# Second mixer: the logarithm of the keys is added to the sums of log gates, so that one exponential gives the decayed keys, and GpSimd has no work there

## The reference, cut to what matters

```python
fq, f_fwd, f_bwd, fi, fog = _split(h @ w_in, ODD_SIZES)
q = _heads(jax.nn.silu(fq), HGRN_HEADS)
for d, f in enumerate((f_fwd, f_bwd)):
    log_f = jnp.logaddexp(jnp.log(lb[d]), jnp.log1p(-lb[d]) + jax.nn.log_sigmoid(_heads(f, HGRN_HEADS)))
    k = -jnp.expm1(log_f)
    dirs.append(_directional_scan(q, k, i, log_f, n_ctx, reverse=(d == 1)))
...
G = jnp.cumsum(gc, axis=2)                     # in _chunk_gla, gc = log_f
decay = jnp.exp(jnp.where(tri, G[:, :, :, None, :] - G[:, :, None, :, :], -jnp.inf))
scores = jnp.einsum('bhik,bhjk,bhijk->bhij', qc, kc, decay)
```

## Time and profile before

| | |
|---|---|
| median of 3 runs | 2525.53 us (2525.48 to 2527.56) |
| span of the profiled execution, first to last instruction | 2523.3 us |
| the difference, what lies around the span | 2.2 us, taken against the median, since the profiled execution has no other time of its own |
| PE, DVE, ACT, POOL busy over the span | 92%, 60%, 42%, 9% |
| the eight heads of the changed stage | 885 to 1175 us of the span |
| mean granted TensorE clock | 0.970 of 2.4 GHz |

### The profile page before, as it was taken

The page is one execution under the profiler, slowest core; times in us unless marked ns, Lnnn a source line. Parts: engine busy times, 40 slices in busy tenths (PEclk is TensorE's granted clock), DMA queues, the critical chain, the costliest instruction groups (busy, mean ns, idle before and its releaser), DMA issues.

```text
span 2523.3 us, 35620 instructions
## 1 busy us (share of the span) xinstructions
PE 2326.2 (92%) x14882; PEld 1850.7 (73%) x14882; DVE 1510.6 (60%) x2358; ACT 1068.3 (42%) x1808; POOL 224.7 (9%) x302
## 2 busy tenths in 40 slices
PE   6987788999998988887999997988999999998999
PEld 3854456888885867766999782336888888878999
DVE  6337655656565487777555515554666565995554
ACT  4244444322234445554445525544332333444543
POOL 0001200000000033322000002110110200000110
PEclk9988988999999999998999999999999999999999
DMA  7154542444432454433554223342444434434453
GB/s 276 68 210 167 213 187 86 142 142 157 159 117 84 134 167 159 142 134 105 187 181 168 77 88 134 134 167 86 142 142 156 145 123 184 177 131 156 168 200 118
DMA packets 175280, 372.80 MB, mean 148 GB/s; under 512 B 8432, under 2 KB 101872, under 8 KB 160784
## 3 DMA queue, kind: packets, MB, share of 16 engines
q1 hardware_dynamic: 175120, 370.53, 42.2%
HBM read 340.07 MB, written 30.44 MB: 147 GB/s over the span
## 4 chain that ended last, share of the span: by engine, by line
PE 75%; DVE 11%; ACT 7%; issue 3%; DMA 2%; POOL 1%; SPq 0%; DVEq 0%; ACTq 0%; POOLq 0%
PE ps L169 74%; DVE sb_R L200 3%; ACT sb_R L252 2%; DVE sb_WP L200 1%; PE ps L179 1%; DVE sb_cst L214 1%; ACT sb_R L258 1%; DVE sb_H L200 1%; DVE sb_cst L200 1%; ACT L245 1%; DMA sb_slot<-mod_w 1%; DVE sb_R L229 1%; DMA sb_slot<-even_w_in 1%; DVE sb_X L217 1%; DVE sb_R L217 1%
## 5 line engine op out<-in xcount | busy, mean ns | idle before, releaser
L169 PE MATMUL ps<-sb_HP,sb_WP 128*128 128x512 f32 (+1 forms) x5736 | 1084.6, 350 | 32.7 <-DVE sb_HP L200 27.6
L169 PEld LDWEIGHTS ps<-sb_HP,sb_WP 128*128 128x128 f32 x5736 | 920.7, 192 | 180.4 <-DVE sb_HP L200 24.6
L200 DVE TENSOR_TENSOR sb_WP<-sb_slot,sb_WP 128x1024 fp32r<-128x1024 f32 x380 | 471.5, 1245 | 593.6 <-ACT sb_WP L258 593.3
L258 ACT ACTIVATE sb_WP<-sb_slot 128x1024 fp32r<-128x1024 f32 x380 | 399.8, 1058 | 724.4 <-PE ps L169 709.3
L169 PE MATMUL ps<-sb_XP,sb_WP 128*128 128x256 f32 (+1 forms) x2976 | 498.2, 330 | 0.3 <-DVE sb_XP L200 0.3
L169 PEld LDWEIGHTS ps<-sb_XP,sb_WP 128*128 128x128 f32 x2976 | 446.0, 191 | 51.8 <-DVE sb_XP L200 0.7
L200 POOL TENSOR_TENSOR sb_R<-sb_R 128x128 f32<-128x128 f32 (+2 forms) x194 | 159.8, 847 | 1546.3 <-ACT sb_R L252 1267.1
L200 DVE TENSOR_TENSOR sb_R<-sb_R 128x256 f32<-128x256 f32 (+3 forms) x398 | 201.2, 540 | 34.1 <-ACT sb_R L252 31.1
L169 PE MATMUL ps<-sb_R 128*32 128x64 f32 (+7 forms) x1768 | 161.4, 288 | 53.8 <-DVE sb_R L200 26.0
L169 PEld LDWEIGHTS ps<-sb_R 128*32 128x32 f32 (+4 forms) x1768 | 113.2, 154 | 110.4 <-issue 68.9
L252 ACT ACTIVATE sb_R<-ps 128x512 f32<-128x512 f32 (+1 forms) x208 | 99.6, 513 | 88.1 <-PE ps L169 83.8
(11 more groups left out here) (149 smaller groups left out, 1863.5 us busy)
## 6 DMA issues: line engine op xcount, KB each, us to landing
sb_slot<-mlp_w SPq DMA_DIRECT2D x32, 2048.0 KB, 8.8
sb_slot<-mod_w SPq DMA_DIRECT2D x22, 2048.0 KB, 8.9
sb_R<-ada_w SPq DMA_DIRECT2D x12, 2048.0 KB, 7.6
sb_slot<-ada_w SPq DMA_DIRECT2D x24, 1024.0 KB, 4.9
sb_slot<-ffn_w_gate SPq DMA_DIRECT2D x22, 1024.0 KB, 5.5
sb_slot<-ffn_w_up SPq DMA_DIRECT2D x22, 1024.0 KB, 8.0
sb_slot<-ffn_w_down SPq DMA_DIRECT2D x10, 2048.0 KB, 7.9
sb_slot<-odd_w_in SPq DMA_DIRECT2D x32, 512.0 KB, 7.3
```

What stands on the lines that cost most here:

```text
L169: return self.e.matmul(out, w, x, start=start, stop=stop, skip_group_check=True)
L200: return BLANK if self.e is None else self.e.tensor_tensor(out, a, b, op)
L258: return self.e.activation(out, a, ACT.Copy) if scale is None else self.e.activation(out, a, ACT.Copy, scale=scale)
```

## The change

The keys of a head are no longer multiplied by an exponential. Since k exp(x) = exp(ln k + x), the logarithm of the keys is made once a head and folded into the sum: K = F - ln k forwards, K = F + ln k backwards. `split_dve` and `keys_dve` subtract K where they subtracted F for the keys, and Exp gives the decayed key itself. In parts:

1. POOL: `keys_pool` of `Levels` (14 multiplications of 128x128 a head) and of `Across` (2 of 128x512 a head) are gone; POOL has no instruction in the stage.
2. ACT: two more activations of 128x512 a head, Ln of the keys with p0 as scale and 2^-60 as bias, behind Ln of the gates.
3. DVE: two more 128x512 subtractions or additions a head (K), behind the two scans and ahead of level 0. The two `tensor_scalar` that make k run over 256 tokens in place of 512, and stand one step earlier, beside the gates. V is written into E's second half.
4. Waits: PE's diagonal blocks wait for k and q, no more for the scans. PE's products wait for E and V in place of U and V; the X multiplications wait for ACT's exponential in place of POOL's product. E has three buffers in turn, freed by the products of three levels before.
5. Small tables (`ex`, `pr`, `mx`) move to another place in memory; a constant is added.

```diff
-            self.levels.append(Levels(p, h, b1, S["q"], ks, S["F"], 2, 2, 1.0, heads, bufs, 3, 5, ready))
-            self.across.append(Across(p, h, b2, S["q"], ks, S["F"], 2, 2, 1.0, WW, QQ, heads, (2, 3), 3, 5))
+            self.levels.append(Folded(p, h, b1, S["q"], ks, S["F"], S["K"], 2, 2, heads, bufs, 3, 5, ready))
+            self.across.append(AcrossFolded(p, h, b2, S["q"], S["F"], S["K"], 2, 2, WW, QQ, heads, (2, 3), 3, 5))
...
+    def diagonal_pe(self, pe):          # Folded
+        nc, tag = self.nc, self.tag
+        pe.wait_ge("k", tag, 1, of="odd.proj")
+        pe.wait_ge("q", tag, of="odd.proj")
...
+    def products_pe(self, pe, m):
+        tag, E = self.tag, self.buf(m)
+        pe.wait_ge("E", tag, m)
+        pe.wait_ge("V", tag, m)
...
+    def split_dve(self, dve, n):
...
+        if n >= 3:
+            self.used(dve, n - 3)
...
+        far = K[:, 0, 0:1, 0:1].offset - F[:, 0, 0:1, 0:1].offset
+        mid = both(F[:, 0, c0, L - 1:L], Fd + 1, [0, L])
+        dve.sub(both(E[:, 0, 0:1], Ez, [1, L]), mid, both(K[:, 0, c0, 0:1], Fd - far, [1, L]))
+        i = dve.sub(both(E[:, 1, L:L + 1], -Ez, [1, L]), both(F[:, 0, c0, L:L + 1], Fd + far, [1, L]), mid)
...
+    def queries_dve(self, dve, m):
+        E = self.buf(m)
+        dve.wait_ge("E", self.tag, m)
+        dve.mul(E[:, 1, :], self.q, E[:, 1, :]).then_inc(*dve.sig("V", self.tag, m))
...
+            act.wait_ge("togo", self.tag, s)          # AcrossFolded.keys_act
+            act.act(w, w, ACT.Exp).then_inc(*act.sig("W", self.tag, s))
...
         e.act(self.g, self.g, ACT.Ln).then_inc(*e.sig("ln", h))
+        for d in range(2):
+            K = S["K"][:, d]
+            e.wait_ge("k", h, d)
+            e.act(K, K, ACT.Ln, scale=self.pr[:, 2 * d, h:h + 1], bias=self.p.v("tiny")).then_inc(*e.sig("lnk", h, d))
...
+        for d in range(2):
+            F, K = S["F"][:, d], S["K"][:, d]
+            e.wait_ge("lnk", h, d)
+            e.wait_ge("F", h, d)
+            (e.sub if d == 0 else e.add)(K, F, K).then_inc(*e.sig("K", h, d))
...
-        pool.on("odd.in").fence(*self.before)
-        for h in range(8):
-            together(self.levels[h].pool(pool.on("odd.mix")), self.cross_pool(pool, h))
+        pass
```

More of the change, by code:

```diff
@@ L1674, in crossed, with __init__, buf, decay_act @@
         e.wait_ge("crossed", self.tag, h, len(self.groups(h)) - 1)
+class Folded(Levels):
+    def __init__(self, p, tag, before, q, ks, F, K, c0, nc, heads, bufs, lo, hi, ready):
+        super().__init__(p, tag, before, q, ks, F, c0, nc, 1.0, heads, bufs, lo, hi, ready)
+        self.K, self.off = K, 0 if before is None else before.off + self.N
+    def buf(self, m):
+        return self.bufs[(self.off + m) % 3]
+    def diagonal_pe(self, pe):
+        nc, tag = self.nc, self.tag
+        pe.wait_ge("k", tag, 1, of="odd.proj")
+        pe.wait_ge("q", tag, of="odd.proj")
+        (pb, sz, P, dg), = self.heads
+        b, ps = pe.take(self.lo, self.hi)
+        for c in range(nc):
+            cs = slice(128 * c, 128 * c + 128)
+            for d, kk in enumerate(dg):
+                i = pe.mm(ps[:, cs], kk[:, cs], self.q[:, cs], d == 0, d == len(dg) - 1)
+        i.then_inc(*pe.sig("diag", tag, 0, bank=b))
+        pe.until(b, "P", tag, -1, 0)
+    def products_pe(self, pe, m):
+        tag, E = self.tag, self.buf(m)
+        pe.wait_ge("E", tag, m)
+        pe.wait_ge("V", tag, m)
+        b, ps = pe.take(self.lo, self.hi)
+        for c in range(self.nc):
+            cs = slice(128 * c, 128 * c + 128)
+            i = pe.mm(ps[:, cs], E[:, 0, cs], E[:, 1, cs], True, True)
+        i.then_inc(*pe.sig("prod", tag, m, 0, bank=b))
+        pe.until(b, "P", tag, m, 0)
+    def decay_act(self, act, n):
+        E = self.buf(n)
+        act.wait_ge("split", self.tag, n)
+        act.act(E, E, ACT.Exp).then_inc(*act.sig("E", self.tag, n))
+    def split_dve(self, dve, n):
+        tag, nc, c0 = self.tag, self.nc, self.c0
+        L, E, F, K = LEVELS[n], self.buf(n), self.F, self.K
+        if n >= 3:
+            self.used(dve, n - 3)
+        elif self.before is not None:
+            self.before.used(dve, self.N - 3 + n)
+        both = lambda x, step, w: bass.AP(x.tensor, x.offset, [list(x.ap[0]), [step, 2], [2 * L, 64 * nc // L], w])
+        Fd, Ez = F.ap[1][0], E.ap[1][0]
+        far = K[:, 0, 0:1, 0:1].offset - F[:, 0, 0:1, 0:1].offset
+        mid = both(F[:, 0, c0, L - 1:L], Fd + 1, [0, L])
+        dve.sub(both(E[:, 0, 0:1], Ez, [1, L]), mid, both(K[:, 0, c0, 0:1], Fd - far, [1, L]))
+        i = dve.sub(both(E[:, 1, L:L + 1], -Ez, [1, L]), both(F[:, 0, c0, L:L + 1], Fd + far, [1, L]), mid)
+        i.then_inc(*dve.sig("split", tag, n))
+    def queries_dve(self, dve, m):
+        E = self.buf(m)
+        dve.wait_ge("E", self.tag, m)
+        dve.mul(E[:, 1, :], self.q, E[:, 1, :]).then_inc(*dve.sig("V", self.tag, m))
@@ new lines, with __init__, keys_dve, keys_act @@
+class AcrossFolded(Across):
+    def __init__(self, p, tag, before, q, F, K, q0, nq, W, Q, heads, chunks, lo, hi):
+        super().__init__(p, tag, before, q, None, F, q0, nq, 1.0, W, Q, heads, chunks, lo, hi)
+        self.K = K
+    def keys_dve(self, dve):
+        self.free(dve)
+        for s in range(2):
+            F, K, w = self.F[:, s], self.K[:, s], self.W[s]
+            w3, end = w.rearrange("p (c x) -> p c x", c=4), (F[:, :, 127:128] if s == 0 else F[:, :, 0:1]).broadcast_to([w.shape[0], 4, 128])
+            (dve.sub(w3, end, K) if s == 0 else dve.sub(w3, K, end)).then_inc(*dve.sig("togo", self.tag, s))
+        for s in range(2):
+            w, x, e = self.W[s], self.W[2 + s], self.W[4 + s]
+            K = lambda c: w[:, 128 * c:128 * c + 128]
+            if s == 0:
+                seq = ((0, K(0), 1), (1, K(1), 2), (2, x[:, 0, :], 2))
+            else:
+                seq = ((0, K(1), 0), (1, K(0), 3), (2, x[:, 0, :], 3))
+            yield
+            dve.wait_ge("W", self.tag, s)
+            dve.wait_ge("whole", self.tag, s)
+            for j, a, b in seq:
+                if j == 2:
+                    dve.wait_ge("X", self.tag, s, 0)
+                dve.ts(x[:, j, :], a, e[:, b:b + 1], ALU.mult).then_inc(*dve.sig("X", self.tag, s, j))
+    def keys_act(self, act):
+        self.free(act)
+        for s in range(2):
+            F, w, e = self.F[:, s], self.W[s], self.W[4 + s]
+            act.wait_ge("togo", self.tag, s)
+            act.act(w, w, ACT.Exp).then_inc(*act.sig("W", self.tag, s))
+            act.act(e, F[:, :, 127 if s == 0 else 0], ACT.Exp, scale=1.0 if s == 0 else -1.0).then_inc(*act.sig("whole", self.tag, s))
@@ L2259, in __init__ @@
         place = Place(p.room, 8192, p.NW - 4096)
-        self.ex, self.pr, self.mx = place(4, 8), place(4, 8), place(2, 8)
-        self.sets = [dict(q=place(TC), og=place(TC), k=place(2, T), F=place(2, 4, 128)) for _ in range(2)]
+        late = Place(lambda at, *shape: shaped(p.cst, at, NCST, shape), NCST - 80)
+        self.ex, self.pr, self.mx = late(4, 8), late(4, 8), late(2, 8)
+        self.sets = [dict(q=place(TC), og=place(TC), k=place(2, TC), F=place(2, 4, 128), K=place(2, 4, 128)) for _ in range(2)]
         self.sg, self.g = place(T), place(2, T)
-        bufs = [(place(2, TC), place(TC), place(TC)) for _ in range(2)]
+        bufs = [place(2, TC) for _ in range(3)]
         PB = place(4 * TC)
```

18 lines of the change are left out of this document (6 added, 12 removed).

## The result

| | before | changed | ratio, 95% interval |
|---|---|---|---|
| first comparison, median of 4 and 4 runs | 2526.55 us (2525.48 to 2528.09) | 2491.86 us (2489.76 to 2501.28) | 0.9895 [0.9873, 0.9918] |
| the same two programs again, 11 and 6 runs | 2517.6 us (2514.51 to 2525.65) | 2500.0 us (2493.19 to 2501.72) | 0.9916 [0.9899, 0.9933] |
| profiled execution, span | 2523.3 us | 2488.0 us, and 2496.9 again | |

The account below looks back on a forecast made before the run. PE and DVE were taken to bound the kernel by waiting for each other in turn. Savings of 6 x 2.4 + 2.0 + 1.65 = 18.05 us took the median from 2525.53 to 2507.5 us, 8-in-10 range 2500 to 2517.

Parts of the forecast that it names:

- S: End of a head's scans on DVE, the zero point for its times; 994.20 us in head 3 before the change.
- p0: PE's products of level 0; forecast at S+4.5 without a stall, or in some heads after a 0.9 us wait.
- p5: PE's products of level 5; forecast 2.5 us earlier, taken as 2.4 a head, with the stretch to the next S unchanged.
- Its central trust: On DVE, the X multiplications are slow because POOL works beside them; the forecast hangs on this.
- lone product: Level 0's query product on DVE, 0.62 us for 0.4; said not to fit the rule of shared ports.
- by rule or by row: Whether the port-blocking rule or the trace's undisturbed durations are used, the forecast sum was claimed to be the same.
- the 1.11: Time in us of the second three X multiplications on DVE, taken as undisturbed; the first three were to fall to it from 2.15.
- Levels 3 to 5: DVE's later levels: 3 and 4 keep their pace and move by 2.0 us; level 5's three products take 1.08 for 1.74.
- p2: PE's products of level 2, set by DVE; forecast to come 1.85 us earlier.
- Another cause for DVE's slowness: Rival, chance 0.08: DVE is not slowed by POOL, K costs 1.3 us and nothing is won; 2525 us.
- the split's subtractions cost more: Rival, chance 0.08: DVE's twelve subtractions reading K and F by a far step each cost 0.26 us more; 2531 us.
- ACT late with the logarithms: Rival, chance 0.05: Ln of the keys ends late, K waits 1 us a head, 8 us are lost; 2515 us.

Follow-up runs that it names:

- the idle POOL work: Changed kernel plus POOL multiplications of constants, in the old ones' places, that nobody reads or waits for; 2522.56 us, ratio to before 1.0012.

## Why the prediction was right, and where it was short

**Direction and mechanism: right.** POOL has no instruction in the stage. The K pair takes 1.27 us (forecast 1.3). The two logarithms of the keys took 1.51 us, more than 2 x 0.63, but ended at 973.08, ahead of S at 974.04. The wait ahead of X is one on ACT, 0.69 (forecast about 0.5). In head 3 p0 comes without a wait, at S + 4.26 (S + 4.5); in head 4, where the matrix-times-vector work stands behind it, p0 comes at S + 3.46 (S + 3.5) behind a wait of 1.07 (0.9). The diagonals do not wait for the scans. From p5 to the next S there are 12.75 us (unchanged, 12.81). In head 7, the wait for the zeros grew from 1.63 to 2.69 in one profile and to 3.69 in the other.

**Its central trust: right, and more so than it says.** "The X multiplications being slow because of POOL" is shown by the idle POOL work, which brings the slowness back without any wait. The Trainium skill, page "SBUF — State Buffer", section "Who interferes with whom", says that the ports shared by VectorE and GpSimd are an exclusive lock. The trace of the kernel before agrees, once the groups of a timeline are taken apart into single instructions. First an X multiplication, then level 0's query product, then a weight remainder and two of level 5's three instructions of 128x256, each beside POOL's instruction:

```profile
1003.70 1.30 POOL L200 TENSOR_TENSOR sb_cst<-sb_cst,sb_R 128x512 f32<-128x512 f32 x1
1003.75 1.34 DVE L214 TENSOR_SCALAR sb_cst<-sb_cst 128x128 f32<-128x128 f32 x1
...
995.80 0.47 POOL L200 TENSOR_TENSOR sb_R<-sb_R 128x128 f32<-128x128 f32 x1 [12.34 <-ACT sb_R L252]
995.92 0.62 DVE L200 TENSOR_TENSOR sb_R<-sb_R 128x256 f32<-128x256 f32 x1
...
1013.45 1.22 DVE L200 TENSOR_TENSOR sb_WP<-sb_slot,sb_WP 128x1024 fp32r<-128x1024 f32 x1
1013.61 1.44 POOL L200 TENSOR_TENSOR sb_R<-sb_R 128x128 f32<-128x128 f32 x1 [2.55 <-ACT sb_R L252]
1014.59 0.74 DVE L200 TENSOR_TENSOR sb_R<-sb_R 128x256 f32<-128x256 f32 x1
1015.01 0.70 POOL L200 TENSOR_TENSOR sb_R<-sb_R 128x128 f32<-128x128 f32 x1
1015.25 0.74 DVE L200 TENSOR_TENSOR sb_R<-sb_R 128x256 f32<-128x256 f32 x1
```

The X multiplication ends 0.08 us behind POOL's instruction, and takes 1.34 where it takes 0.28 alone. Of the 48 in the eight heads 40 began while POOL was at work, and every one ended 0.08 to 0.09 us behind the POOL instruction that was running; the other 8 took 0.27 to 0.28. The query product (0.41 alone) ends 0.28 behind POOL's, and so do both of level 5's. It goes the other way as well: POOL's instruction at 1013.61 ends 0.38 behind the weight remainder that had begun before it, and the one at 1015.01 as much behind the DVE instruction at 1014.59. So the prediction read its lone product wrongly. It said that the rule does not fit, "since POOL was busy much longer than the 0.2 lost"; but the product was held by one POOL instruction, up to 996.26, and not by the pair. It also says that by rule or by row the sum is the same. Laid on every row of POOL, the rule would have marked the 1.11 as disturbed.

**The step that was mis-sized:** "It then takes 1.11 in place of 2.15" and "Levels 3 to 5. Nothing is added; levels 3 and 4 keep their pace." Both took rows of before as undisturbed which POOL disturbed as well; of the 1.11 the prediction says outright "with POOL idle". It was at work at just these places, as its timeline in the kernel before shows:

```profile
1006.50 0.88 POOL L200 TENSOR_TENSOR sb_R<-sb_R 128x128 f32<-128x128 f32 x2 [1.49 <-ACT sb_R L252]
1010.00 1.06 POOL L200 TENSOR_TENSOR sb_R<-sb_R 128x128 f32<-128x128 f32 x2 [2.63 <-ACT sb_R L252]
```

The X groups gave back 1.47 + 0.44 us (2.15 to 0.68, 1.11 to 0.67), and level 4's pair of 128x256 another 0.32 (1.08 to 0.76): 2.2 where the forecast had 1.04. That is 1.2 us more a head, up to 9.6 over eight. By its own points: up to p2 2.17 were won (forecast 1.85), from p2 to p5 1.59 (10.23 to 8.64; forecast about 0.6). The stage's 26.3 to 27.2 us, 8.3 to 9.1 more, stand against the forecast's 18.05. That the first comparison shows 34.7 is partly chance: in the profiled executions 9.6 us of scatter ahead of the stage came on top, and 1.5 went behind it. A head is 31.4 us, not the 32.7 of the prediction's signs, and the X groups take 0.68 and 0.67, not 1.1.

**The rivals.** *Another cause for DVE's slowness* and *the split's subtractions cost more* fell: the idle POOL work alone brings the slowness back, and level 0's four subtractions take 1.43 us in the new form, as they did before. *ACT late with the logarithms* fell with a margin of 0.96 us.

**What stays open.** What sets the granted clock in the first mixer from run to run, and what tells a wait of 1.83 us that the lower clock follows from one that it does not. The 1.5 to 2.6 us lost behind the stage. How much of the folding's 1.4 us a head is work and how much are waits was not taken apart. The waits of about 2.6 us of PE on ACT in sb_R (L258) at the end of the stage are as long as they were and were not tried.

## What to carry to other kernels

A duration from the trace is a duration beside whatever else was running: before a row serves as the undisturbed price, look at what the neighbouring engine did in that very microsecond, and prefer the shortest row of the same form. Where two engines may hold each other up, take the groups apart and compare single ends: a constant distance between them (here 0.08 or 0.28 us) shows which one held the other, where averages show only "slower". An engine at 9% that nobody waits for can cost another one more than its waits do: here 3.8 us of a 35-us head were disturbance and 1.35 were waits, put back in this order. And where the same program scatters by 16 us, measure an edit of 1 or 2 us in its own stage, from its own start to its own end.

## What the runs showed of the hardware

- VectorE and GpSimd held each other up for whole instructions. In the kernel before, a `tensor_scalar` of 128x128 that began while GpSimd was at work ended 0.08 to 0.09 us behind GpSimd's instruction (40 of 40), whether it took 0.46 or 1.34 us by that; alone it took 0.28. Two-input instructions of 128x256 in sb_R ended 0.28 behind it (23 of 26; the other three took their 0.42), alone they take 0.41 to 0.43; the distances of 128x512 ended 0.55 behind it (15 of 16), in 0.94 for 0.68. So an instruction that was held had done its first part by then and lacked only the rest. The turns do not always alternate: with the idle POOL work, a GpSimd instruction that began at 978.81 took 2.44 us beside a weight remainder of 1.22 and three products at their undisturbed 0.42. Averages hide all this: 523 to 593 ns for 280, 928 to 931 for 683. GpSimd's pair of 128x128 took from 0.88 to 2.10 us within one head of the kernel before.
- A wait of TensorE of 1.83 or 2.32 us was followed in some heads by work at the lower of its two levels: 12 matmuls in 3.89 us for 2.35 (granted clock 0.56), 16 in 3.21 for 1.90 (0.57). Then a wait costs nearly twice its length. In heads 3 and 6 of the same kernel a wait of 1.83 was followed by work at 1.00. In the kernel before, the 12 matmuls of 3.14 us in head 2, behind a wait of 2.17, ran at 0.72. Waits of up to 1.1 us in the changed kernel left the granted clock at 1.00 in each of heads 1 to 4.
- On ScalarE, Ln with a scale and a bias from memory took 800 ns a 128x512 on average, a plain Exp of that size 629.
